# Where the gather's row indices are set in the expert loop, and two moves in its last passes

## The reference

```python
def expert_block(args):                      # one block of tokens of one expert
    tok, wb, e = args
    xb = t_pad[tok]                          # gather rows of tokens
    yb = swiglu(xb, w_e_gate[e], w_e_up[e], w_e_down[e])
    return yb * wb[:, None]
routed = jax.ops.segment_sum(yb, slot_tok)   # scatter-add by token
out = x + gate * rmsnorm(routed + shared)
```

## Time and profile before

| | |
|---|---|
| median of three runs | 1004.16 us |
| profiled execution: device time | 1006.02 us |
| its span, first to last instruction | 1004.2 us |
| PE busy | 933.3 us, 93% |
| DVE, ACT, POOL busy | 532.7, 325.5, 451.0 us |
| mean granted PE clock | 0.98 of full |
| bytes moved by DMA | 299.69 MB, mean 298 GB/s |

### The profile page before, as it was taken

One profiled execution on the slowest core, in us unless ns is written; L12 is line 12 of the kernel. 1 busy time (PEld: TensorE's weight loads), 2 busy tenths in 40 slices (PEclk: granted clock), 3 DMA queues, 4 the chain that ended last, 5 costly groups with the idle time before them and its releaser, 6 DMA issues.

```text
span 1004.2 us, 14499 instructions
## 1 busy us (share of the span) xinstructions
PE 933.3 (93%) x4307; PEld 403.4 (40%) x4308; DVE 532.7 (53%) x767; ACT 325.5 (32%) x541; POOL 451.0 (45%) x342
## 2 busy tenths in 40 slices
PE   3899999999999999979999979997999999999684
PEld 1644444677455543323333323332333333333231
DVE  1337888786266954535545435453454454444257
ACT  4112222577246412222322322222233233222232
POOL 0312432000000148855677664775577777666211
PEclk9999999999999999989999999998999999999988
DMA  9955452430325979999979999999999999999875
GB/s 370 354 209 209 168 198 73 180 126 1 126 84 210 361 250 349 394 392 390 397 267 375 405 402 391 403 397 372 404 369 372 387 363 382 381 363 349 270 289 157
DMA packets 68448, 299.69 MB, mean 298 GB/s; under 512 B 21518, under 2 KB 22514, under 8 KB 39361
## 3 DMA queue, kind: packets, MB, share of 16 engines
q1 hardware_dynamic: 41522, 261.16, 65.3%
q0 software_dynamic: 25840, 35.98, 13.6%
q10 hardware_dynamic: 1056, 2.18, 0.6%
HBM read 284.78 MB, written 62.91 MB: 346 GB/s over the span
## 4 chain that ended last, share of the span: by engine, by line
PE 53%; DMA 29%; issue 7%; DVE 4%; SPq 3%; POOL 2%; ACT 1%; ACTq 0%; POOLq 0%; DVEq 0%
PE psum L1271 15%; PE psum L1023 12%; DMA wring<-in_w_e_down 10%; PE psum L1283 7%; DMA wring<-in_w_e_up 6%; DMA xg<-h_rows,gidx 6%; PE psum L1114 3%; PE psum L1094 3%; DMA ring<-in_w_in 3%; DMA expert_sums<-xres,sidx 3%; PE psum L1085 2%; PE psum L1061 2%; PE psum L1233 2%; DMA wring<-expert_sums 2%; PE psum L999 2%
## 5 line engine op out<-in xcount | busy, mean ns | idle before, releaser
L1271 PE MATMUL psum<-wring,xres 128*64 (+1 forms) x1664 | 374.7, 604 | 18.6 <-DVE wring L1751 17.5
L583 POOL DMA_INDIRECT xg<-h_rows,gidx x208 | 258.8, 1244 | 114.8 <-issue 88.6
L1271 PEld LDWEIGHTS psum<-wring,xres 128*64 128x64 f32 x1664 | 119.7, 140 | 235.7 <-issue 235.5
L1283 PE MATMUL psum<-wring,rows 128*64 x416 | 187.1, 592 | 2.7 <-ACT rows L834 1.7
L1283 PE MATMUL psum<-rows 128*64 128x512 f32 x416 | 187.1, 592 | 0.0
L1755 DVE STREAM_TRANSPOSE xres<-xg 128x1024 f32<-128x1024 f32 x52 | 106.9, 2056 | 72.0 <-issue 46.7
L1751 DVE COPY wring<-wring 128x1536 f32 x104 | 123.9, 1233 | 26.0 <-SPq L465 24.5
L1787 DVE SCALAR_TENSOR_TENSOR rows<-rows,slot_w,psum 128x256 f32<-128x256 f32 x52 | 24.9, 480 | 203.8 <-ACT rows L895 126.1
L891 ACT COPY xres<-psum 128x1024 f32<-128x1024 f32 x52 | 52.6, 1012 | 178.1 <-PE psum L1283 124.8
L834 ACT COPY rows<-wring 128x1024 f32 x104 | 103.6, 1046 | 7.4 <-PE psum L1283 7.2
L1283 PEld LDWEIGHTS psum<-wring,rows 128*64 128x64 f32 x416 | 56.8, 137 | 120.6 <-issue 120.5
(11 more groups left out here) (273 smaller groups left out, 901.2 us busy)
## 6 DMA issues: line engine op xcount, KB each, us to landing
wring<-in_w_e_gate SPq DMA_DIRECT2D x64, 1024.0 KB
wring<-in_w_e_up SPq DMA_DIRECT2D x64, 1024.0 KB
wring<-in_w_e_down SPq DMA_DIRECT2D x64, 1024.0 KB
ring<-in_w_ada SPq DMA_DIRECT2D x20, 1024.0 KB, 4.6
wring<-expert_sums SPq DMA_DIRECT2D x8, 1024.0 KB, 13.2
ring<-in_w_in SPq DMA_DIRECT2D x3, 2048.0 KB, 27.2
heads<-in_w_ada SPq DMA_DIRECT2D x4, 1024.0 KB, 22.7
ring<-in_w_out SPq DMA_DIRECT2D x1, 4096.0 KB, 12.9
```

What stands on the lines that cost most here:

```text
L583: pool.indirect_dma_start(xg[q][:, 256 * s:256 * s + 256], None, hrows, bass.IndirectOffsetOnAxis(gidx[:, q, s:s + 1].bitcast(U32), 0), bo ...
L1271: last = pe.matmul(pp[2][SUB * g:SUB * g + SUB, 512 * q:512 * q + 2 * F] .rearrange("p (u f) -> p u f", u=2), xT[:, q, k, SUB * g:SUB * g ...
L1283: last = pe.matmul(pp[q][SUB * g:SUB * g + SUB, 512 * m:512 * m + 512], hTb[:, j, SUB * g:SUB * g + SUB], cur_d[:, j, 512 * m:512 * m + 51 ...
```

## The change

Three edits. (1) The copy of the gather's indices moves from DVE, where it stood right behind the transpose, to ACT, at the head of `open_pass`, with the wait for the transpose in front of it; POOL no longer waits for the transpose itself. (2) In the written-out end of ACT, `block_silu` of pass 50 moves ahead of `keep_y` of pass 49. (3) In the written-out end of DVE, `add_sums(0)` moves ahead of the last `keep_hidden`.

```diff
@@ POOL
-            def gather(p, q, set_by, turned=None):
-                if turned is not None:
-                    pool.wait_ge(s_xte, turned)
+            def gather(p, q, set_by):
                 pool.wait_ge(s_gi, set_by)
...
                 for q in range(2):
-                    gather(i + (q + 2), q, i + (q + 2), i + (q + 1))
+                    gather(i + (q + 2), q, i + (q + 2))
                     scatter(i + (q - 2), q, ysb[:, q], i + (q + 1))
@@ ACT
+            def gather_index(p, q):
+                act.wait_ge(s_xte, p - 1)
+                act.copy(gidx[:, q, :], slot_g[:, bass.ds((p + 1) * 4, 4)]).then_inc(s_gi, 1)
...
             def open_pass(p, q):
+                gather_index(p + 2, q)
                 w = down_weights(p)
                 block_silu(q, p + (NT + 1))
                 return w
...
+            block_silu(0, passes(NT - 1))
             keep_y(passes(NT - 1), 1, landed(-2))
             scatter_index(more * 2 + (LEAST - 3), 1)
             copy_down(*down_weights(more * 2 + (LEAST - 2)))
-            block_silu(0, passes(NT - 1))
@@ DVE
-            def gather_index(p, q):
-                dve.tensor_copy(gidx[:, q, :], slot_g[:, bass.ds((p + 1) * 4, 4)]).then_inc(s_gi, 1)
...
                     turn_block(1 - q, i * 32 + 64 * (q + 1))
-                    gather_index(i + (q + 3), 1 - q)
                     gated(i + q, q, i + (q + NT + 1), i + (q + NT))
...
+                if k == -1:
+                    add_sums(0)
                 if k != -3:
                     keep_hidden(q, passes(NT + 2 + k), passes(NT + 1 + k))
...
-            add_sums(0)
             add_sums(1)
```

More of the change, by code:

```diff
@@ L613, in _ @@
             for p in range(2):
-                gather(p + 2, p, p + 2, p + 1)
+                gather(p + 2, p, p + 2)
                 scatter(p - 2, p, arow[:, 3], p + 1)
@@ L1778, in _ @@
             turn_block(0, 64)
-            gather_index(2, 0)
             extra = dve.value_load(ntab[0:1, 0:1], min_val=0, max_val=MAXB - 1 - E)
@@ L1836, in _ @@
                     turn_block(1 - q, n_gathered)
-                if k == -4:
-                    gather_index(more * 2 + (LEAST - 1), 1)
                 gated(more * 2 + (LEAST + k), q, passes(NT + 1 + k), passes(NT + k))
```

## The result

The changed kernel takes 1009.27 us (median of five runs, 1007.88 to 1012.25) against 1004.13 us (1001.18 to 1006.02) for the kernel before on the same chip: a ratio of 1.0061, 95% interval 1.0040 to 1.0084. It is slower by 5 us. The direction was forecast, the size was not: 1040 us stood against it. The profiled execution took 1007.20 us, a span of 1005.4 us and 1.8 us around it. It is 2.1 us under its kernel's median, and the profile before (1006.02) is 1.9 us over its own, so these two traces differ by 1.2 us only: the loop is 5.9 us longer, the end 3.4 us shorter, and the loop starts 1.2 us earlier.

A forecast was written before the change was run, and what follows sets the result against it. The prediction took the weights' DMA stream to bound the kernel as much as PE. Loop +38.9, edit 2 -5 and edit 3 +2 gave +36 on 1006.0, 1042, less 1.9 for the median: 1040 us, range 1001 to 1085.

The forecast's parts named there:

- Edit 1, the delays: Expert loop: index set 10.2 us later, gather and scatter issued behind it, 13.5 us from keep_y to the scatter's last issue.
- The cycle 2T = 13.5 + S: Expert loop: two passes of T each last 13.5 us plus scatter landing S; T = 12.17 us in 44 passes.
- The size of S: Scatter's landing time after its last issue in the loop: forecast 10.8 us, shrinking from S0 in the DMA's idle time.
- S0 = 14: Assumed scatter landing in us beside the full weights' stream, chosen between 9.1 and 19.0.
- 16.3 of the last undelayed scatter: Late in the loop: scatter 40 landed at most 16.3 us after its issue, with nobody waiting; used to choose S0.
- The ends of my bound: Loop with S0 from 9.1 to 19.0: T from 11.27 to 12.68 us, loop change from -0.7 to +61.3 us.
- Edit 2: -5 forecast: ACT's end: block_silu(50) first removes PE's wait, and keep_y(49) comes 23 us behind gate_up 49; -5 us (-8 to 0).
- Edit 3: +2 forecast: DVE's end: add_sums(0) first delays the last keep_hidden, mostly covered, but PE's clock drops after idling; +2 us (0 to +3).
- The landing shrinks by itself: Rival, loop: later issue falls where the stream pauses, S 9.2, T about 11.3, total about 1004 us; chance 0.12.
- Never pauses: Rival, loop: stream never pauses for POOL, S stays 18 to 19, T 15.8, +198, about 1200 us; chance 0.05.
- The clock: Rival, PE in the loop: uneven stalls repeatedly lower the granted clock, +43 us, together 1083 us; chance 0.13.
- my two signs of being wrong: Loop: gate_up's starts staying at 10.74 us, or the scatter landing in 8 us beside a DMA share of 1.0.

The follow-up runs named there:

- e7: Kernel before, index copy left on DVE, but POOL's gather in the loop also waits for copy_down's end on ACT: 1007.27 us, ratio 1.0064.
- e11: Kernel before, unchanged, run and profiled a second time: 1001.18 us, ratio 0.9988.
- e9: Changed kernel, but POOL waits until a gather has landed before it issues the scatter: 1147.21 us, ratio 1.1450.
- e5: Changed kernel with the index copy on ACT moved ahead of copy_down, some 2 us earlier: 1005.46 us, ratio 1.0036.
- e6: Changed kernel with the index copy on ACT moved behind block_silu, so gathers are issued later: 1029.24 us, ratio 1.0282.
- e1: Kernel before with the index copy on ACT (edit 1) alone: 1006.76 us, ratio 1.0044.
- e4: Changed kernel with POOL issuing the scatter ahead of the gather in the loop: 1015.39 us, ratio 1.0131.
- e8: Kernel before with only two of the four issues of each gather: 977.69 us, ratio 0.9767.
- e10: Changed kernel with each weight load moving half its bytes from the seventh expert on: 975.58 us, ratio 0.9744.
- after: Profile of the changed kernel itself, all three edits against the kernel before: median 1009.27 us, ratio 1.0061.
- e12: Kernel before with edits 2 and 3 and without edit 1: 1001.27 us, ratio 0.9985.

## Why the prediction was right in its sign and wrong in its size

**Edit 1, the delays: right.** Index, gather and scatter came when the working said, 13.5 us from `keep_y` to the scatter's last issue. `e7` shows that this delay alone makes edit 1.

**The cycle 2T = 13.5 + S: it exists, but it doesn't set the pace.** Late in the loop S is 9.9 and T would be 11.70; measured 11.71. This proves little: where `keep_y` waits for a scatter, S is by its definition what two passes leave beside the 13.5 us. In the middle ACT waits for scatters too, but PE's passes are 10.7 to 11.0 us there except at the stalls for weights, which the kernel before has as well. The working let the cycle bind in 44 passes; it reaches PE in some 14, from 35 on, by way of DVE, where `gated` stands behind the transpose that waits for the gather.

**The size of S: this is the step that failed.** I took S0 = 14, a scatter's landing beside a full stream, "nearer to the 16.3 of the last undelayed scatter than to 9.1", for the whole loop, and had it shrink only in idle time of the DMA. Measured, S is 9.4 at a share above 0.9, with no idle time at all. The ends of my bound held (9.1 gave a loop of 549.9, measured 556.4), but the value within it was chosen badly. The 16.3 for scatter 40 was not far from its landing (15.0 us for the same scatter in `e11`), but both it and the 19.0 came from the last passes, where landings had been growing since scatter 28. In the middle the kernel before landed its scatters in 8.3 us beside a share of 1.0, and the change left that as it was (8.7). So for most of the 44 passes there was no landing of 14 us to begin with.

What grew late was the backlog of POOL's own queue. In `e11` a scatter of passes 34 to 46 landed 7.0 us after the gather ahead of it had landed, and its issue had ended 8.6 us before that moment; in the changed kernel it is 7.0 and 2.8. `e9` takes the queue away (7.9), the changed kernel leaves one gather in it (9.4), and `e5` and `e6` move the issue by 2 us and more and see S move against it (11.6; 8.3 to 9.0).

With S of 9.0 to 9.9 in the working, the sum for the loop is 5 x 10.8 + 44 x 11.4 = 555.6, +5 where +38.9 stood; this pair of profiles has +5.9. That they agree so well is partly luck: the 550.5 is the longest of five loops of this code, and the 11.4 is a mean over stalls that the cycle does not cause. (Two sums are off by a tenth: the terms of the 13.5 add up to 13.4, those of the 31.4 to 31.3.)

**What the loop's loss is.** The landings give the pace at which POOL's queue is emptied late in the loop, from scatter 34 to scatter 46: 11.5 to 11.6 us a pass in the five profiles of the loop before, and 11.8 in the changed kernel, `e1`, `e4` (the other order) and `e5`, 11.9 in `e7`. It depends little on when or in what order POOL issues. With less to move (`e8`, `e10`) it is 10.8, and the queue keeps up with PE. Before, PE's late passes took 10.74 us against this, and the debt was held in POOL's queue, where landings grew to 15 and 19 us without PE waiting. The changed kernel has no room for a debt, so PE runs at the queue's pace (11.71), and pays 11.6 us in twelve passes. It gets part back, because the weights are further ahead at the end (SP issues the last loads at 927.82 us, where it did so at 933.04) and scatter 47 isn't late: the end is 3.4 us shorter. Both kernels move 299.69 MB. When the issue is later still, nothing is left to shrink and every pass pays (`e6`, +28 us).

Over all profiles the sum is steadier than in the one pair. Passes 0 to 34 take 384.9 us in the mean of the five without edit 1's timing (380.1 to 388.5) and 382.5 in the three with it (`after`, `e1`, `e7`: 380.9 to 384.5), which is within the spread; passes 34 to 49 take 161.4 and 174.3; the three ends (75.0 to 76.4) are 4.3 us under the mean of the two profiles of the kernel before (79.8 and 80.0). That is +10.5 in the loop, -4.3 at the end, +6 in all, where the timed ratios of the same three give 1.0044 to 1.0064. Why the DMA empties POOL's queue at this pace beside a full stream is not shown by any run.

**Edit 2: -5 forecast, the end measured -3.4, but not by this edit.** `e1` has the short end without it (75.0). Beside the kernel before it is worth 2.3 us of the end in one profile (77.5 against 79.8) and nothing in `e12` (80.0). The forecast took `keep_y` 49 at 23 us behind gate_up 49; in the changed kernel it is 952.33 - 929.04 = 23.3, and that is edit 1's doing, by the shorter queue.

**Edit 3: +2 forecast; no cost shows.** The fold behind it ends 32.5 us after the last landing and is late by 0.30 us. From that landing to the end of the span it is 1005.4 - 961.6 = 43.8 us, before 1004.2 - 960.5 = 43.7. The slow clock that I feared is there: down(51), after PE's idle time of 6.85 us, takes 6.2 us instead of 3.6. The first sums came 7.7 us after the landing instead of 9.7, and that covered it.

**The rivals.** "The landing shrinks by itself" gave 1004 (999 to 1009) with S of 9.2 and T of 11.3, and came nearest of all; I gave it 0.12. Its reason did not hold, as the share stayed at 1.0 and the landings of the middle had been short before. "Never pauses" had the right share and the backlog's S. The clock fell only around a few stalls (0.83 from 680 to 700 us, 1.00 from 820 to 920), not in a rhythm. Of my two signs of being wrong each came in part: gate_up's starts stayed at 10.74 in most passes up to 34, and the scatter landed in 8.7 us beside a share of 1.0.

On the Trainium skill's rule that each DMA engine serves the queues with work in turn ("DMA: Bandwidth & Descriptors", section "Queues, rings and completion order"): the trace agrees in that a scatter beside a full stream lands in 7.9 us and beside little in 2.9. What I drew from it, an S of 18 for good and passes of 15.8 us, was wrong: the rule is on the turns between queues, and 18.2 - 7.9 = some 10 of the 18 us went with the backlog in POOL's own queue.

## What to carry to other kernels

A landing counted from the issue is the transfer's own time plus its queue's backlog. Before using one as a cost under a new timing, look at what the same queue issued before it, and read it at several places of the loop: the landings that somebody waited for are the longest ones, and here they were all late. In this kernel, with the DMA full, a later issue cost only a part of its delay, once, as long as there was backlog to take it from (10 us later, some 5 us in all); beyond that it cost in every pass (`e6`). And where a kernel seems to run faster than its DMA, look for the queue whose landings grow: here its slack was a buffer that was partly paid back at the end, so the change that took the slack moved the loss, and the sum moved little.

## What the runs showed of the hardware

- In `e9`, four indirect gathers of 128 rows x 1 KB land 2.0 us after the last issue beside a DMA share below 0.5 and 6.7 us above 0.9; the two transfers of a scatter 2.9 and 7.9 us.
- Beside the full stream, late in the loop, POOL's queue landed one gather and one scatter in 11.5 to 11.9 us in ten profiles of five schedules, whether PE's passes took 10.74 us or 11.7.
- Half the weights' bytes (`e10`) shortened a scatter's mean landing from 9.1 to 5.2 us, but a gather's only from 6.0 to 5.2.
- 8.7 MB less of 299.7 MB, in small gathered pieces, took 24 us off (`e8`), 2.3% of the time for 2.9% of the bytes.
- The same loop at the same code took 542 to 551 us in five profiles: a spread of 9 us, larger than the 5.9 us by which the changed loop differs from one of them. What carries the verdict is the timed ratios and that all three profiles with edit 1's timing (556.4, 558.5, 555.4) lie above all five.
